# Triangular inverse by levels: updating products on half the columns, and subtractions on half the columns

## The reference

```
lower = jnp.where(strict, jnp.einsum('bnhid,bnhjd->bnhij', kb, kc) * decay, 0.0)
amat = lower + jnp.eye(c, dtype=lower.dtype)
rhs = jnp.concatenate([vb, kb * jnp.exp(gc)[..., None]], axis=-1)
sol = lax.linalg.triangular_solve(amat, rhs, left_side=True, lower=True, unit_diagonal=True)
...
def step(s, xs):
    u_i, w_i, attn_i, qg_i, kd_i, gl_i = xs
    v_new = u_i - jnp.einsum('bhcd,bhde->bhce', w_i, s)
    o = jnp.einsum('bhcd,bhde->bhce', qg_i, s) + jnp.einsum('bhij,bhje->bhie', attn_i, v_new)
    s = s * gl_i[..., None, None] + jnp.einsum('bhcd,bhce->bhde', kd_i, v_new)
    return s, o
```

## Time and profile before

| | before |
|---|---|
| median of 3 runs | 1357.07 us (1356.89 to 1358.92) |
| profiled execution, time and span | 1360.63 us, span 1357.2 us |
| TensorE busy, share of the span | 95% |
| weight loads (PEld) | 48% |
| VectorE, ScalarE | 32%, 20% |
| mean granted TensorE clock | 0.991 of full speed |

### The profile page before, as it was taken

The page is one execution under the profiler, slowest core; times in us unless marked ns, Lnnn a source line. Parts: engine busy times, 40 slices in busy tenths (PEclk is TensorE's granted clock), DMA queues, the critical chain, the costliest instruction groups (busy, mean ns, idle before and its releaser), DMA issues.

```text
span 1357.2 us, 16458 instructions
## 1 busy us (share of the span) xinstructions
PE 1283.2 (95%) x6361; PEld 653.5 (48%) x6361; DVE 433.8 (32%) x812; ACT 271.2 (20%) x503; POOL 32.2 (2%) x73
## 2 busy tenths in 40 slices
PE   7999989989999999999999999989999999999996
PEld 6777678756655434344344343424434343443433
DVE  2545565275124321232213312122221212322123
ACT  3466552130022111011110111101111010111102
POOL 5000000001000000000000000000000000000000
PEclk9989999999999999999999999999999999999999
DMA  9623200126586999999999999999999999999993
GB/s 274 182 62 99 94 32 1 62 70 210 224 347 248 422 429 427 429 428 428 428 429 428 430 427 430 427 429 428 428 429 428 429 428 429 428 430 427 430 428 158
DMA packets 61885, 447.76 MB, mean 330 GB/s; under 512 B 7637, under 2 KB 30249, under 8 KB 37276
## 3 DMA queue, kind: packets, MB, share of 16 engines
q1 hardware_dynamic: 59836, 440.34, 78.8%
q0 software_dynamic: 2016, 6.99, 1.5%
HBM read 442.30 MB, written 5.02 MB: 330 GB/s over the span
## 4 chain that ended last, share of the span: by engine, by line
PE 65%; DMA 28%; DVE 5%; ACT 1%; issue 1%; DVEq 0%; SPq 0%; ACTq 0%
PE bank L671 30%; DMA ring<-in_w_gate_up_dram 27%; PE bank L618 14%; PE bank L1078 6%; PE bank L1009 2%; PE bank L1172 1%; PE bank L874 1%; PE bank L685 1%; PE bank L886 1%; PE bank L882 1%; PE bank L1151 1%; PE bank L633 1%; DVE qkgb L1989 1%; PE bank L662 1%; PE bank L1144 0%
## 5 line engine op out<-in xcount | busy, mean ns | idle before, releaser
L671 PE MATMUL bank<-ring,zgb 128*64 128x512 f32 x2560 | 563.5, 594 | 42.5 <-DMA ring<-in_w_gate_up_dram 34.2
L671 PEld LDWEIGHTS bank<-ring,zgb 128*64 128x64 f32 x2560 | 180.1, 137 | 422.6 <-issue 339.2
L1980 DVE COPY zgb<-bank 128x512 f32<-128x512 f32 x32 | 22.1, 691 | 602.5 <-PE bank L671 602.5
L618 PE MATMUL bank<-hTb,ring 128*128 128x320 f32 x640 | 178.3, 437 | 0.8 <-DVE hTb L1575 0.8
L618 PEld LDWEIGHTS bank<-hTb,ring 128*128 128x128 f32 x640 | 121.3, 191 | 52.7 <-issue 4.6
L671 PE MATMUL bank<-ring,oABb 128*64 128x512 f32 x512 | 113.4, 595 | 0.0
L1507 ACT COPY zgb<-bank 128x512 f32<-128x512 f32 x32 | 18.7, 586 | 427.7 <-PE bank L671 427.7
L1078 PEld LDWEIGHTS bank<-oABb,h2b 128*128 128x128 f32 (+1 forms) x768 | 88.7, 196 | 13.0 <-issue 13.0
L1078 PE MATMUL bank<-oABb,h2b 128*128 128x128 f32 (+1 forms) x768 | 94.1, 284 | 0.0
L1517 ACT COPY hTb<-bank 64x512 f32<-64x512 f32 x64 | 37.1, 580 | 251.4 <-PE bank L671 250.4
L1151 PE MATMUL bank<-hTb 128*128 128x512 f32 x136 | 68.2, 606 | 0.0
(11 more groups left out here) (382 smaller groups left out, 880.0 us busy)
## 6 DMA issues: line engine op xcount, KB each, us to landing
ring<-in_w_gate_up_dram SPq DMA_DIRECT2D x128, 2048.0 KB, 30.5
ring<-in_w_down_dram SPq DMA_DIRECT2D x64, 2048.0 KB, 35.3
ring<-in_w_in_dram SPq DMA_DIRECT2D x22, 1024.0 KB, 5.5
ring<-in_w_o_dram SPq DMA_DIRECT2D x4, 1024.0 KB, 12.5
ring<-in_w_up_a_dram SPq DMA_DIRECT2D x2, 1024.0 KB, 4.9
ring<-in_w_up_b_dram SPq DMA_DIRECT2D x2, 1024.0 KB, 5.2
out_dram<-ring POOLq DMA_DIRECT2D x1, 2048.0 KB, 13.1
xbuf<-in_x_prompt_dram SPq DMA_DIRECT2D x2, 512.0 KB, 4.1
```

Source lines behind the costliest of these rows:

```text
L618: mm = pe.matmul(o[0:m, 0:TOK], w[:, k, c0:c0 + m], rhs[:, k, :], start=(k == 0), stop=(k == kk - 1))
L671: mm = pe.matmul(o[64 * f:64 * f + 64, 0:width], lhs, w[f] if isinstance(w, list) else w[:, width * f:width * f + width], start=start, sto ...
L1980: link(V.tensor_copy(pre[:, 1, :], bank[PRE[1]][:, :]), pre_done[1], n * 2 + (x + 1))
```

## The change

Of the two blocks in a pair, only one changes in T_ and one in TT: at level b, Y is subtracted from the first b columns of each 2b columns of T_, and Z from the second b columns of each 2b columns of TT. In the other columns the products are zero. After the change only the columns that can change are moved through TensorE: `half` picks every other run of b columns of the moving operand (64 of 128 columns, 32 of 64 on tile 2). The products come to lie next to each other in PSUM, and `less_product` subtracts them from the picked columns of T_ or TT, which lie in runs of b with gaps of b. X, the stationary operands, the copies, the mask products, the order of the instructions on each engine and the waits are as before; VectorE's 14 + 11 subtractions (Z and Y) remain as many, with half the elements.

```
+            def half(v, b, t):
+                return v.rearrange("p (c t b) -> p c t b", t=2, b=b)[:, :, t, :]
...
                     if b != levels_of(s)[-1]:
-                        o = p3(take(f"Y{s}{b}"), HEADS, 128)
+                        o = p3(take(f"Y{s}{b}"), HEADS, n // 2)
                         for h in range(HEADS):
-                            mm = pe.matmul(o[0:n, h, 0:n], TT[0:n, s, h, 0:n], X1[0:n, s, h, 0:n], start=True, stop=True)
+                            mm = pe.matmul(o[0:n, h, :].rearrange("p (c b) -> p c b", b=b), TT[0:n, s, h, 0:n],
+                                           half(X1[0:n, s, h, 0:n], b, 0), start=True, stop=True)
                         done(mm, f"Y{s}{b}")
-                    o = p3(take(f"Z{s}{b}"), HEADS, 128)
+                    o = p3(take(f"Z{s}{b}"), HEADS, n // 2)
                     for h in range(HEADS):
-                        mm = pe.matmul(o[0:n, h, 0:n], X1[0:n, s, h, 0:n], TT[0:n, s, h, 0:n], start=True, stop=True)
+                        mm = pe.matmul(o[0:n, h, :].rearrange("p (c b) -> p c b", b=b), X1[0:n, s, h, 0:n],
+                                       half(TT[0:n, s, h, 0:n], b, 1), start=True, stop=True)
                     done(mm, f"Z{s}{b}")
...
+            def less_product(dst, s, n, b, t, name):
+                o = p3(full(dve, name), HEADS, n // 2)[0:n].rearrange("p h (c b) -> p h c b", b=b)
+                v = dst[0:n, s, :, 0:n].rearrange("p h (c t b) -> p h c t b", t=2, b=b)[:, :, :, t, :]
+                free(TTo(v, v, o, ALU.subtract), name)
...
                     if not final:
                         level(s, i + 1, lt_ready)
-                        o = p3(full(dve, f"Y{s}{b}"), HEADS, 128)
-                        free(TTo(T_[0:n, s, :, 0:n], T_[0:n, s, :, 0:n], o[0:n, :, 0:n], ALU.subtract), f"Y{s}{b}")
-                    o = p3(full(dve, f"Z{s}{b}"), HEADS, 128)
-                    free(TTo(TT[0:n, s, :, 0:n], TT[0:n, s, :, 0:n], o[0:n, :, 0:n], ALU.subtract), f"Z{s}{b}")
+                        less_product(T_, s, n, b, 0, f"Y{s}{b}")
+                    less_product(TT, s, n, b, 1, f"Z{s}{b}")
```

## The result

Twenty executions of the changed kernel took 1360.91 us in the median, from 1355.51 to 1377.01. Twenty of the kernel before on the same chip took 1356.98, from 1355.25 to 1359.03. The ratio is 1.0025, with a 95% interval of 1.0014 to 1.0037. The change makes the kernel slower by 0.25%, where 1355.4 us, no measurable change, was forecast.

What follows compares the result with a forecast made beforehand. In the inverse (193 to 231 us) TensorE bounds, waiting for VectorE at X1. Three times 0.52 us (1.56) plus 0.11 gives 1.67 us, from the median 1357.07 to 1355.4 us; range 1352.9 to 1359.5.

Steps and rivals of the forecast that it cites:

- The pace of TensorE's groups: Y and Z products: 128-column weight loads set the pace, so halving 176 matmul records' columns gains 0.
- the subtractions: VectorE, after Y and Z: 128x512 becomes 128x256, 687 ns becomes 425 ns, despite runs with gaps.
- the three waits before X1: Levels 16, 32, 64: TensorE waits 0.63 us for VectorE's last subtraction before the second tile's X; this goes.
- 0.12 us came back at Y0: First tile's Y of the next level: a new 0.11 us wait for ScalarE's copy of X0.
- the 0.117 us of L654: TensorE pace evidence: 48 records of 24 columns take 5.60 us, 0.117 each, so fewer columns go no faster.
- Does it reach the end?: After 231 us: work releases what follows, the expert weight stream starts earlier, and the 1.67 us is kept whole.
- Nothing shows: Rival: subtractions keep 0.69 us, waiting is ScalarE's, or later work takes the gain; 1357.1; 0.15 including one or two falls.
- C: Experiments' theory, not the prediction's: the expert stage's weight stream loses something, with the difference behind 430 us.
- The clock rival: Y and Z: fewer columns lower TensorE's clock, 1.56 us a fall, up to 1363.2; three falls or more 0.09.

Runs made afterwards that it cites:

- the late load: Kernel before, with SyncE's load of panel w_up_b held back until product ga4 is complete: 1368.5 to 1371.7 us in four executions, ratio 1.0087 [1.0072, 1.0103].

## Why the prediction was wrong

**Right:** the inverse itself. The pace of TensorE's groups stayed 0.89 us, so halved columns gave 0; the subtractions take 421 ns (425 forecast), and 421 to 423 at runs of 2; the three waits before X1 went and 0.12 us came back at Y0 (0.11 forecast). The inverse gained 1.78 us (1.67 forecast), and in the profiled execution its clock stayed at 1.00 from 197 us on. One reading was loose: the 0.117 us of L654 is a mean of 32 records with loads of 128 columns, 0.111 us apart at full clock, and 16 with loads of 64 columns behind the fall at 73.5 us. The conclusion, that 24 columns do not go below 0.111, holds by the 32.

**The step that failed** is "Does it reach the end?": "What follows 231 us is released by work and not by a clock", "so the saving is kept whole". In the short executions the gain is given back in a fall of the clock near 270 us (1.69 us) which the kernel before does not have, and which comes with the earlier arrival and not with the columns. That gives 0, not -1.67. The prediction had read the very records in front of that product (L922 and L924, 270.5 to 273.3 us, clock at 1.00) as a sign that 64 columns do not bring the clock down; moved 1.4 us ahead, the clock falls at their end. The other half of the executions lose more than the gain: four of the twenty by the clock in the levels, the others by what is open below. "Later work takes the gain" stood under the rival "Nothing shows", at 1357.1: that is what the short executions did. The first expert wait of the profiled execution starts 0.28 us later than before, at 706.78 for 706.50, so C is not needed for it.

**The clock rival was right that fewer columns cost clock, and wrong in form and size.** It was priced at 1.56 us a fall, at most 6.1 us, with a chance of 0.09 for three falls or more. What the one long trace with 64 columns shows is not new falls but a low clock that lasts some 20 us longer than with 128, and costs 9 us. It happens in some executions and not in others: with halved products 22 of 75 executions had a mean clock of 0.983 or less, with 128 columns none of the 125 whose clock is recorded (four with the late load, at 0.986 to 0.987, are the lowest). The chance was put on one time; the kernel has several.

**The order of w_up_b and the stores was on no list.** Its margin, 1.11 us, could have been read in the trace of before (load issued at 317.28, stores at 318.39). In the halved subtractions alone it costs 9 us in the traced long execution, and 7 of 11 executions have that time. No trace shows it in the changed kernel itself.

**Open:** the group at 1362 us, and the one at 1377, are in no trace; the second fits both causes added, as with the halved products at 1376. The first group is 5 of the 10 long executions that set the median at 1360.91, so part of the 0.25% has no cause shown. Which falls come in which execution is not explained either: why a long execution has them at 295 and 312 us where a short one has them at 286 and 303 was not tried.

**A version without the two causes of long executions** is the halved subtractions with full products and the stores held back: 0.9993 [0.9984, 1.0003] of before. None of its 12 executions is long, unlike the change's, and it cannot be told from the kernel before. The two traces of short executions that these subtractions have without the hold lose the gain at 269 us as the change does.

## What to carry to other kernels

A stretch made shorter moves all that follows against the moments at which the clock falls, and against other queues; before a saving is carried to the end, look in the trace for the next stretch of few moving columns behind which a fall could come, and for pairs of transfers that are only a microsecond apart, and pin the order of such a pair with a wait. Where the weight load sets TensorE's pace, halving the moving columns gives nothing and may hold the clock down. Measure many executions: a median over groups is the time of none of them.

## What the runs showed of the hardware

- A TensorE that the profile shows busy without a pause (19.00 of 19.00 us) stayed at half clock for that time with 64 moving columns in Y and Z on 128-column loads, from a start at half clock (one trace). With 128 columns, from the same start, it was back at full clock by 199.2 us (three traces).
- A 1 MB load took 5.2 us when issued 1.11 us ahead of 2 MB of stores, 6.5 us when 1.03 us behind their start, and 16.70 us when 1.90 us behind it. There the two queues sent packets in turn, 471 to 465 in 8 us, of some 4 KB and 2 KB.
- VectorE's subtraction with runs of 2 elements costs what runs of 128 cost, 421 to 423 against 425 ns for 128x256.
